# A transformer block pair with a convolution branch: the order of each conv layer, its projections and the engine of its convolution

## The reference, cut to what matters

```
for l in range(2):
    mod = silu(c) @ ada_w[l] + ada_b[l]              # shift, scale, gate
    h = rms_norm(x, norm_g[l]) * (1 + scale) + shift
    z = h @ w_in[l]                                  # 2048 x 4928
    q_lat, kv_lat, k_rope, mla_gate, conv_in, conv_gate = split(z)   # 512, 256, 64, 1024, 2048, 1024
    ... q, k, v from q_lat, kv_lat; norms, rotation; causal attention, 8 heads ...
    mla_out = attn * silu(mla_gate)
    u_val, u_gate = split(conv_in + glu_b[l])        # 1024 columns each
    u = u_val * sigmoid(u_gate)
    u = causal_depthwise_conv(u, dw_w[l], dw_b[l])   # 31 taps, 1024 channels
    u = silu(layer_norm(u, conv_ln_g[l], conv_ln_b[l]))
    u = u @ w_pw[l] + b_pw[l]                        # 1024 x 1024
    conv_out = u * silu(conv_gate)
    y = concat([mla_out, conv_out]) @ w_out[l]       # 2048 x 2048
    x = x + gate * y
```

## Time and profile before

| what | before |
|---|---|
| median of 3 runs | 2102.03 us (2101.68 to 2104.43) |
| the profiled execution: its own time | 2113.76 us |
| its span, first to last instruction | 2112.0 us |
| instructions | 25133 |
| PE busy | 2011.7 us (95%) |
| DVE busy | 1469.5 us (70%) |
| ACT busy | 1075.8 us (51%) |
| POOL busy | 394.8 us (19%) |
| mean granted TensorE clock | 0.974 |

### The profile page before, as it was taken

The page is one execution under the profiler, slowest core; times in us unless marked ns, Lnnn a source line. Parts: engine busy times, 40 slices in busy tenths (PEclk is TensorE's granted clock), DMA queues, the critical chain, the costliest instruction groups (busy, mean ns, idle before and its releaser), DMA issues.

```text
span 2112.0 us, 25133 instructions
## 1 busy us (share of the span) xinstructions
PE 2011.7 (95%) x9332; PEld 1662.0 (79%) x9332; DVE 1469.5 (70%) x1708; ACT 1075.8 (51%) x1607; POOL 394.8 (19%) x380
## 2 busy tenths in 40 slices
PE   7999999999999999999999898799999898799998
PEld 5788888888888888888888787677778787677787
DVE  4686777776767777777755589974455589874454
ACT  5455445455443544444444555664644565665642
POOL 0222232000000000000000024862100034852101
PEclk9999999999999999999999999989999999989999
DMA  6777877888889888888865554444346455434344
GB/s 207 249 241 239 267 240 236 293 273 291 294 278 306 285 283 299 295 291 280 306 205 188 154 163 135 130 120 125 111 139 209 140 161 146 124 113 134 120 153 146
DMA packets 207761, 441.96 MB, mean 209 GB/s; under 512 B 14661, under 2 KB 23127, under 8 KB 207639
## 3 DMA queue, kind: packets, MB, share of 16 engines
q1 hardware_dynamic: 207459, 439.93, 64.6%
q10 hardware_dynamic: 180, 0.43, 0.1%
HBM read 438.20 MB, written 2.10 MB: 208 GB/s over the span
## 4 chain that ended last, share of the span: by engine, by line
PE 38%; issue 38%; DVE 13%; POOL 5%; ACT 4%; SPq 1%; DMA 1%; ACTq 0%; DVEq 0%; POOLq 0%
PE P L684 11%; PE P L685 10%; PE P L686 10%; DVE CA L1005 6%; DVE WL L1008 5%; POOL ST L1324 1%; PE P L448 1%; ACT WH L992 1%; PE P L565 1%; PE P L564 1%; POOL QK L1346 1%; SPq L1479 1%; PE P L606 1%; PE P L555 1%; DMA RAW<-in_sb_w_qkv_dram 1%
## 5 line engine op out<-in xcount | busy, mean ns | idle before, releaser
L1008 DVE TENSOR_TENSOR WL<-RAW,WH 128x1024 fp32r<-128x1024 f32 (+2 forms) x648 | 809.9, 1256 | 426.3 <-ACT WH L992 425.5
L992 ACT ACTIVATE WH<-RAW 128x1024 fp32r<-128x1024 f32 (+2 forms) x648 | 672.0, 1043 | 616.5 <-PE P L686 479.7
L684 PE MATMUL P<-WH,AH 128*128 128x512 f32 (+1 forms) x1536 | 617.2, 402 | 37.1 <-DVE WL L1008 33.2
L685 PE MATMUL P<-WL,AH 128*128 128x512 f32 (+1 forms) x1536 | 604.9, 394 | 0.0
L686 PE MATMUL P<-WH,AL 128*128 128x512 f32 (+1 forms) x1536 | 604.3, 393 | 0.0
L684 PEld LDWEIGHTS P<-WH,AH 128*128 128x128 f32 x1536 | 296.3, 193 | 105.6 <-DVE WL L1008 35.0
L684 PE MATMUL P<-WH,BH 128*128 128x512 f32 x896 | 352.4, 393 | 0.0
L686 PE MATMUL P<-WH,BL 128*128 128x512 f32 x896 | 349.3, 390 | 0.0
L685 PE MATMUL P<-WL,BH 128*128 128x512 f32 x896 | 349.0, 389 | 0.0
L686 PEld LDWEIGHTS P<-WH,AL 128*128 128x128 f32 x1536 | 296.0, 193 | 61.3
L685 PEld LDWEIGHTS P<-WL,AH 128*128 128x128 f32 x1536 | 296.8, 193 | 56.1
(11 more groups left out here) (252 smaller groups left out, 1538.4 us busy)
## 6 DMA issues: line engine op xcount, KB each, us to landing
RAW<-in_ada_w_dram SPq DMA_DIRECT2D x192, 512.0 KB, 5.0
RAW<-in_w_in_dram SPq DMA_DIRECT2D x144, 512.0 KB, 3.7
RAW<-in_mlp_w_in_dram SPq DMA_DIRECT2D x128, 512.0 KB, 4.7
RAW<-in_mlp_w_out_dram SPq DMA_DIRECT2D x128, 512.0 KB, 5.3
RAW<-in_sb_w_qkv_dram SPq DMA_DIRECT2D x96, 512.0 KB, 4.9
RAW<-in_w_out_dram SPq DMA_DIRECT2D x64, 512.0 KB, 4.1
RAW<-in_sb_w_o_dram SPq DMA_DIRECT2D x32, 512.0 KB, 5.5
RAW<-in_w_pw_dram SPq DMA_DIRECT2D x16, 512.0 KB, 3.8
```

What stands on the lines that cost most here:

```text
L684: e.matmul(o, xh, wh, start=st and k == 0, stop=False)
L685: e.matmul(o, xh, wl, start=False, stop=False)
L992: e.activation(WH[:, n % NH, 0:size], RAW[:, i % NR, 0:size], ACT.Copy).then_inc(w_high, 1)
L1008: return e.tensor_tensor(o, x, h.bitcast(F32), ALU.subtract)
```

## The change

- **Order of a layer.** z chunks 0, 1, 4, 5, 2, then up 0, 6, 3, up 1, 7, up 2, 8, up 3, 9.
- **Value and gate in one chunk.** Chunks 0 to 3 each hold 256 value columns and the 256 gate columns that belong to them, so that two tiles of the convolution can start after one chunk. Such a unit is loaded by two transfers (`halves`), one for each 128 rows, with runs of 1 KB; the waits on the slots count transfers (`landed`).
- **Output projection in two halves.** `oa` sums w_out over rows 0 to 1023 (attention), `ob` over the rest (convolution), each in 4-unit groups: 16 units `oa`, 8 units `p`, 16 units `ob`. `o_add` now runs eight times a layer, all on DVE.
- **Convolution on DVE alone.** The ACT products, the POOL sums, `PB` and `POOL_CT` go. 248 taps over 89 units, from unit 9 of the layer to unit 97, in pairs of tiles that alternate.
- **Layer norm.** DVE sums over the 8 tiles first (`over_tiles`, a strided `tensor_reduce`, four a layer), so that PE has 2 matmuls for the mean and 4 for the variance; mean and scale are read straight from PSUM. `SQL` has 4 places. The norm stands at units 98 to 107 instead of 67 to 72.

```diff
+        self.halves = g[0] == "z" and c < 4
...
-        zc = [(1856, 512), (2880, 512), (2368, 512), (3392, 512), (0, 512), (512, 320), (832, 512), (1344, 512), (3904, 512), (4416, 512)]
+        zc = [(1856, 512), (2112, 512), (2368, 512), (2624, 512), (0, 512), (512, 320), (832, 512), (1344, 512), (3904, 512), (4416, 512)]
...
+            def o_units(part, c):
+                for k in range(8 * part, 8 * part + 8, 2):
+                    unit((("oa", "ob")[part], l), c, w_o, k * 128, k, 2, 512 * c, 512, k % 8 == 0, k % 8 == 6)
+                d = done[(("oa", "ob")[part], l), c]
+                after[d].append(("o_add", l, part, c))
...
-            for c in range(7):
+            for c in (0, 1, 4, 5, 2):
                 z_units(c)
-            for g in range(3):
-                up_units(g)
-                z_units(7 + g)
+            up_units(0)
+            z_units(6)
+            z_units(3)
+            up_units(1)
+            z_units(7)
+            up_units(2)
+            z_units(8)
+            up_units(3)
+            z_units(9)
             zend.append(len(units))
...
-            o_units(0, (0, 2), p0)
-            p_units(0, p1)
-            o_units(0, (4,), p0)
-            p_units(1, p1)
-            o_units(0, (6, 8, 10), p0)
-            o_units(1, (0, 2), p1)
-            o_units(0, (12, 14), p0)
-            o_units(1, range(4, 16, 2), p1)
-            o_units(2, range(0, 16, 2), p0)
-            o_units(3, range(0, 16, 2), p1)
             for c in range(4):
+                o_units(0, c)
+            for c in range(2):
+                p_units(c)
+            for c in range(4):
+                o_units(1, c)
...
-            for half in range(2):
-                s = b + 19 + 24 * half
-                for k in range(31):
-                    after[s + k - k // 4].append(("conv", l, half, k))
-            s = b + 67
-            after[s].append(("ln_mean", l))
+            for i in range(248):
+                after[b + 9 + i * 89 // 248].append(("conv", l, i))
+            after[b + 60].append(("ln_sum", l, 0))
+            s = b + 98
+            after[s].append(("ln_sum", l, 1))
+            after[s + 1].append(("ln_mean", l))
+            after[s + 2].append(("ln_centre", l))
             after[s + 4].append(("ln_var", l))
-            after[s + 5].append(("ln_scale", l))
+            after[s + 5].append(("ln_rstd", l))
+            after[s + 6].append(("ln_scale", l))
+            for cp in range(4):
+                after[s + 6 + cp].append(("ln_act", l, cp))
...
+            def conv(l, i):
+                ct, k = 2 * (i // 62) + i % 2, i % 62 // 2
+                x, w = UT[:, ct, k:k + 256], DW[:, l, ct, k:k + 1]
...
+                    e.wait_ge(*conv_d.at(l, ct, k - 1))
+                    fma(CA[:, ct, :], x, w, CA[:, ct, :], ALU.mult, ALU.add).then_inc(*conv_d.up(l, ct, k))
+
+            def over_tiles(o, x):
+                return e.tensor_reduce(o, x.rearrange("p c n -> p n c"), AXX, ALU.add)
...
+                    if u.halves:
+                        dst = dst.rearrange("p k (s n) -> p k s n", s=2)
+                        for k in range(2):
+                            r = u.r0 + 128 * k
+                            src = u.src[r:r + 128, u.c0:u.c0 + 1280].rearrange("p (s n) -> p s n", n=256)[:, 0:5:4, :]
+                            e.dma_start(dst[:, k, :, :], src).then_inc(raw[i % NR], 16)
+                        return
```

More of the change, by code:

```diff
@@ L147, in build @@
         UT = put("UT", [128, 8, 286], off=oS)
-        LNS = put("LNS", [128, 4, 256], off=oS)
-        SQL = put("SQL", [128, 2, 512], off=oS + 4 * K)
+        SQL = put("SQL", [128, 4, 512], off=oS)
         o2 = oS + 9152
@@ L168, in build @@
         BR = put("BR", [1, 1024], off=oA + 28 * K)
-        UV = put("UV", [128, 2, 512], off=oBH)
-        UG = put("UG", [128, 2, 512], off=oBH + 4 * K)
+        U1 = put("U1", [128, 2, 512], off=oBH + 4 * K)
         CA = put("CA", [128, 8, 256], off=oBH + 8 * K)
@@ L286, in z_units @@
                 after[d].append(("z_evict", l, c))
-                if c in (1, 3):
-                    for i in range(4):
-                        after[d + 1 + i // 2].append(("glu", l, 2 * (c - 1) + i))
+                if c < 4:
+                    after[d + 1] += [("glu", l, 2 * c), ("glu", l, 2 * c + 1)]
                 if c in (4, 5):
@@ L365, in build @@
+            after[s + 9].append(("gate_act", l))
         NU = len(units)
@@ L378, in build @@
         assert not adas
+        landed, transfers = [], [0] * NR
+        for i, (kind, n) in enumerate(items):
+            transfers[i % NR] += 2 if kind == "w" and units[n].halves else 1
+            landed.append(16 * transfers[i % NR])
         ada_of = lambda l, pc, kt: 96 * l + 16 * pc + kt
@@ L594, in ln_mean @@
                 pb = bank(("lnm", l))
-                for ct in range(8):
-                    e.wait_ge(*(conv_p if ct in POOL_CT else conv_d).at(l, ct, 30))
-                    m = e.matmul(pb[:, 0:256], ONE, CA[:, ct, :], start=ct == 0, stop=ct == 7)
+                for part in range(2):
+                    e.wait_ge(*ln_d.at(l, "sum", part))
+                    m = e.matmul(pb[:, 0:256], ONE, FB[:, 2, part * 256:(part + 1) * 256], start=part == 0, stop=part == 1)
                 m.then_inc(*T.filled(("lnm", l)))
@@ L601, in ln_var @@
                 pb = bank(("lnv", l))
-                for cp in range(4):
-                    e.wait_ge(*ln_a.at(l, cp))
-                    for i in range(2):
-                        for t in range(2):
-                            m = e.matmul(pb[:, t:t + 1], SQL[:, cp % 2, i * 256 + t * 128:i * 256 + (t + 1) * 128], ONE[:, 0:1],
-                                         start=cp == 0 and i == 0 and t == 0, stop=cp == 3 and i == 1 and t == 1, skip_group_check=True)
-                    if cp < 3:
-                        m.then_inc(*ln_seen.up(l, cp))
+                for part in range(2):
+                    e.wait_ge(*ln_d.at(l, "squares", part))
+                    for t in range(2):
+                        m = e.matmul(pb[:, t:t + 1], FB[:, 3, part * 256 + t * 128:part * 256 + (t + 1) * 128], ONE[:, 0:1],
+                                     start=part == 0 and t == 0, stop=part == 1 and t == 1, skip_group_check=True)
                 m.then_inc(*T.filled(("lnv", l)))
@@ L1236, in ln_mean, with ln_sum, ln_centre @@
+            def over_tiles(o, x):
+                return e.tensor_reduce(o, x.rearrange("p c n -> p n c"), AXX, ALU.add)
+            def ln_sum(l, part):
+                for ct in range(4 * part, 4 * part + 4):
+                    e.wait_ge(*conv_d.at(l, ct, 30))
+                over_tiles(FB[:, 2, part * 256:(part + 1) * 256], CA[:, 4 * part:4 * part + 4, :]).then_inc(*ln_d.up(l, "sum", part))
+            def ln_centre(l):
                 e.wait_ge(*T.ready(("lnm", l)))
-                e.tensor_scalar(LNS[:, 0, :], T.ap(("lnm", l))[:, 0:256], 1.0 / 1024, None, ALU.mult).then_inc(*T.drained(("lnm", l)))
@@ L1245, in ln_var, with ln_rstd @@
+                for i in range(2):
+                    e.wait_ge(*ln_a.at(l, 2 * i + 1))
+                    sq = SQL[:, 2 * i:2 * i + 2, :].rearrange("p a (c n) -> p (a c) n", c=2)
+                    over_tiles(FB[:, 3, i * 256:(i + 1) * 256], sq).then_inc(*ln_d.up(l, "squares", i))
+            def ln_rstd(l):
                 e.wait_ge(*T.ready(("lnv", l)))
```

181 lines of the change are left out of this document (60 added, 121 removed).

## The result

The changed kernel takes 2021.49 us (median of 4 runs, 2019.50 to 2023.17), the kernel before, timed beside it, 2103.23: the ratio is 0.9608, with an interval of 0.9592 to 0.9625. It is faster by 81.7 us; 2031 was forecast, with 1998 to 2070 as the range. The profiled execution took 2023.17, its span 2021.4. Between the two profiled executions there are 90.6 us, more than between the medians, because that of before lay 10.5 above its median and that of the changed kernel 1.7 above its own.

The account below looks back on a forecast made before the run. Losses lay in DVE, the attention chain through POOL, and small PE work with a low clock. Layer 0: 44.3 + 64.5 + 190.2 + 123.7 + 13.8 = 436.5 against 474.0; both layers save 70.9 off 2102.03: 2031 us, range 1998 to 2070.

Parts of the forecast that it names:

- Convolution on DVE alone: Each layer: 248 taps at 0.40 are 99 us of DVE against 93 before, provided POOL is quiet.
- Chunks 0 and 1: Layer start: 43.5 of units and 0.8 for two tile inputs, 44.3 us; loading units in halves costs nothing.
- Chunks 4, 5, 2: PE needs 59.5 us, DVE 58.8; with 5 added for lag, 64.5, ends 59.5 and 72.
- The four up groups: With chunks 6 to 9 and 3: POOL's chain sets a period of 41.7, four times, plus 23.4: 190.2 us.
- rival B: The stalls go and the clock stays up: periods of 37.4, 22 us less a layer, 1987; chance 0.12.
- `oa`, `p`, `ob`: Output projection with the norm: 40 units at 108.8, small work and 3 of waiting, 123.7 us; ends 120 and 130.
- The strided sum: Norm's DVE sums over 8 tiles, stride 1 KB: 1.2 us each like a contiguous reduce, other end double.
- Join: From layer 0 to layer 1: 13.8 us, unchanged, since the last chunk's operations are the same.
- A: DVE stays the bound: periods of 46.7, chunks 4, 5, 2 take 70; 2082, halfway 2057; chance 0.14.
- C: Slower: alternating two tiles exposes tap latency; decides from 0.73 us a tap, at 0.8 kernel takes 2140; chance 0.04.
- D: DVE's load moves, PE's wait does not: only some 15 us a layer saved, 2072; chance 0.06.
- E: Each tap starts when the last has ended: 0.47 a tap, 17 us more DVE a layer, 2045; chance 0.04.

Follow-up runs that it names:

- e1b: Changed kernel with three of the eight convolution tiles given back to ACT (product) and POOL (sum): 2036.7 us.
- e2b: Kernel before with all eight convolution tiles on DVE, still in two bursts of 24 units: 2087.9 us.
- e3b: Changed kernel with its 248 taps pressed into three bursts of 25, 13 and 13 units: 2063.4 us.
- e5: Changed kernel with the layer norm's sums over tiles back on PE, without DVE's four strided sums: 2025.9 us.
- e11: Kernel before with all tiles on DVE, convolution over 62 units and norm from unit 82 in place of 67: 2060.6 us.
- e6: Changed kernel with the taps of one tile after another in place of alternating pairs of tiles: 2031.7 us.
- e7: Changed kernel with convolution over 86 units, norm begun three units earlier with looser steps, gate activation five units earlier: 2014.8 us.
- e10: Kernel of e7 with the norm's mean and what follows, and each attention step, one unit later: 2002.8 us.
- e4b: Changed kernel with 240 of 248 taps a layer left out, so it computes something else: 2027.7 us.
- e9: Kernel of e4b with each low part in the layers cut into two DVE operations of 512 columns: 2017.3 us.

## Why the prediction was right, and where it was off

**Convolution on DVE alone: right.** Taps start 0.40 apart with POOL quiet, and the 66 convolution operations of chunks 4, 5, 2 take 27.52 us, 0.42 each. "Throughout" did not hold: over layer 0 the 240 taps after each tile's first keep DVE busy for 109.9 us, 0.46 each, since POOL's attention work runs beside some. e1b and e2b show that POOL's sums made the tap dear, and that by itself the engine was the smaller part of the gain, 15 to 17 of some 82 us. The prediction gave the engine and the spread one sum; without the spread 42 us of the gain are lost (e3b).

**Chunks 0 and 1**: 45.4 for 44.3, at a clock of 0.98. PE is busy in all of it, so the units in halves cost nothing that shows; no run loads them otherwise. **Chunks 4, 5, 2**: 61.1 for 64.5. Of the 5 us of lag that I added 1.6 came.

**The four up groups: the step that failed.** "41.7 four times and 23.4 for chunk 3: 190.2" became 36.5, 36.9, 40.2, 39.6 and 23.8, together 177.0, so 13.2 too much. "The chain through POOL goes on setting the period" held in two groups out of four, and there only for 1 to 2 us. Two terms were mis-sized. The waits: length less PE's busy time is 2.6 in the earlier trace rows, four times that is 10.5, and in the four periods now 0.0 + 0.2 + 2.2 + 1.3 = 3.7. And PE's own time, 39.1 a period in the earlier trace rows at a clock of 0.96, 37.4 on average now at 1.00; besides, the first two periods don't carry the tail of an earlier group. I took a period under a low clock as the price of a period, and rival B's argument ("the clock stays up") was the right one for this stretch.

**`oa`, `p`, `ob`: forecast too short.** They took 131.1 us for 123.7. The waits were 3.3, as the 3 said. The rest is the last group's tail in `oa`, 3.0 of PE's time which I had counted nowhere, the norm's operations at 3.1 for 2.1, and the clock: a mean of 0.94 over 86.5 us is some 5 us of work at full speed, an estimate. The row of PE's wait for the sums of squares, and the one behind it:

```profile
1493.50:1497.60 4.10, 2.55 (x15) 1.92 (x15) 3.18 (x2) 4.07 (x4) 0.00 (x0) 1.00 0.02 9
1497.70:1501.10 3.40, 3.40 (x10) 2.63 (x10) 2.96 (x3) 2.30 (x3) 0.00 (x0) 0.54 0.06 10
```

PE is busy for 2.55 of 4.10 us, and then runs at a granted 0.54, most of it at the lower level, 1.2 GHz. The 3 us of waiting had no term for the clock. That the wait brought the clock down is not shown, though. In the same kernel a low stretch comes 1.3 us after the four single-row matmuls of the bias, with no wait in front of it (first line), and none comes after the wait of 1.3 us for POOL's k rows that ends at 1440.35 (second line). In e5 PE is busy without a gap from 1480 on, and the clock falls at 1498.2 all the same, while the one-column matmuls of the variance run (third line):

```profile
1517.80:1521.90 4.10, 4.10 (x12) 3.20 (x12) 4.07 (x6) 1.69 (x3) 0.00 (x0) 0.58 0.46 149
1440.40:1450.00 9.60, 9.60 (x50) 7.54 (x50) 9.10 (x16) 3.56 (x5) 0.00 (x0) 1.00 0.58 188
1498.20:1505.00 6.80, 6.80 (x23) 5.93 (x24) 1.30 (x2) 0.00 (x0) 0.00 (x0) 0.50 0.73 235
```

The strided sum, priced at 1.2 with 2.4 as its other end, came at 2.0. The Trainium skill, SBUF — State Buffer, Specifications (TRN2), has a penalty for each new 16-byte line; the trace agrees in direction, 2.0 against the 1.2 of a contiguous reduce. The two also differ in how many results they write, 256 against 8, so that the penalty alone is not shown to be the cause.

**Join**: 13.8, as forecast.

**Rivals.** A (DVE stays the bound) fell: PE waits 0.4 us for low parts in layer 0. B was half true, in the periods and not in `oa`. C fell: 0.40 a tap in pairs, and even one tile at a time costs only 10 us. D fell, with e1b, e2b, e3b and e11: the load's place and engine move 15 to 42 us. E fell: a tap starts 0.40 after the last, before that one's 0.48 are over; only a tap that reads the result of the one just before it comes later, 0.52 (e6). The Trainium skill, VectorE: DVE Perf Modes, section "The DRAIN you can't avoid", has the next operation wait for an empty pipe, and adds that one which is not held starts earlier. The prediction used the first half alone; the taps in pairs, 0.40 apart at 0.48 long, agree with the second. The taps of e6 wait for a semaphore of the one before and so test neither.

**The sum**: 8.1 us too much in layer 0 and 10.6 in layer 1. That the forecast still missed the median by only 9.5 is partly luck. It subtracted 70.9, where the profiled executions differ by 90.6, and it did so from the median of the kernel before, while its rows came from an execution that was a long one: 9 of the 90.6 are that. Within the sum 7.4 too little for `oa`, `p` and `ob` made up for part of the 13.2 too much for the up groups.

**Where the 82 went**, as far as the runs part it: engine 15 to 17, spread 27 (old order, with the norm's move) to 42 (new order), norm's sums some 4, order of chunks some 4. From e11 to the changed kernel there are 39 us. Chunk 9, with the norm in it, is 14 us a layer longer in e11, and `oa` pays a part of that in the changed kernel (3.3 of waits, 2.4 of operations and the clock). The norm's place was not moved by itself, nor was the projection unmixed or value and gate joined by itself, so how the 39 split stays open; and the effects overlap, so that they need not add up.

A part of all of these came through the clock. Its mean over an execution was 0.971 to 0.980 in the runs of the kernel before beside the experiments, and is 0.990 to 0.994 now. From 0.977 to 0.990 some 28 us of PE's work at full speed come back, an estimate of the most that it can be, since part of the time at the lower level holds no work in either kernel. The prediction had the clock only inside the price of a period.

## What to carry to other kernels

When an engine is near its limit in one stretch and has room in the next, try to spread its work evenly before moving part of it to another engine: here the spread was worth 27 to 42 us and the engine 15 to 17, and buffers of a few steps did not bridge a burst. Put a serial chain (norm, softmax) where the bounding engine has steps to run through, and allow it one step more than it needs (e7, e10). And price a repeated period from a stretch in the state in which the new one will run, clock included: the price taken at 0.96 was 39.1 us of PE, and 37.4 at 1.00.

## What the runs showed of the hardware that was not expected

Where both have work queued, the starts of POOL's and DVE's operations alternate, one of each, and the length of the neighbour counts, not only how busy it is. A POOL operation of 0.47 us took 0.65 beside a tap (0.48 long where POOL is quiet), 0.91 beside half a low part (0.69) and 1.44 beside a whole one (1.21). So less work on DVE made POOL's chain longer (e4b: 8.1 us of waiting for its k rows in a layer against 2.5), and the same work in shorter operations made it shorter (e9: 1.9, and 2017.3 us against 2027.7). Four low parts in a row beside POOL took 5.42 us; three of 1.13 and a last one of 1.2, as where POOL is quiet, would be 4.6.
